# Rounding the high parts of the weights in a GpSimd DMA queue instead of on ScalarE

## The reference

```
h = concat(meta, x)
mix = hybrid_mixer(rmsnorm(h), ...)        # 16 stick-breaking heads, 4 retention heads, two gates, then @ w_out
h = h + rmsnorm(mix)
h = h + rmsnorm((silu(a) * b) @ w_ffn_out)  # a, b = split(rmsnorm(h) @ w_ffn_in), width 2816
...
second block: 5 input projections, a causal convolution of 3 taps and one of 31 taps,
layer norm, @ w_out_2, then a second SwiGLU of width 2816
```

## Time and profile before

| | before |
|---|---|
| device time, median of 3 runs | 2078.57 us (2076.77 to 2080.33) |
| span of the profiled execution | 2078.3 us |
| PE busy | 2016.7 us (97%) |
| DVE busy | 1095.9 us (53%) |
| ACT busy | 710.0 us (34%), of it 267.3 us high parts of weights |
| POOL busy | 14.6 us (1%) |
| DMA | 157.5 MB, 76 GB/s mean |

### The profile page before, as it was taken

The page is one execution under the profiler, slowest core; times in us unless marked ns, Lnnn a source line. Parts: engine busy times, 40 slices in busy tenths (PEclk is TensorE's granted clock), DMA queues, the critical chain, the costliest instruction groups (busy, mean ns, idle before and its releaser), DMA issues.

```text
span 2078.3 us, 25213 instructions
## 1 busy us (share of the span) xinstructions
PE 2016.7 (97%) x10194; PEld 1667.7 (80%) x10194; DVE 1095.9 (53%) x1346; ACT 710.0 (34%) x845; POOL 14.6 (1%) x10
## 2 busy tenths in 40 slices
PE   7999999989999999999999999999999999999996
PEld 6878888778989888887768888887898768888884
DVE  3454645544363544636564445454699664544445
ACT  5554655523332323224342222223333442222222
POOL 0000000000000000000000000000000000000000
PEclk9989999989999999999999999999999999999998
DMA  4010101012212222221312222222122112222221
GB/s 166 21 41 21 61 20 61 22 70 99 73 61 81 71 90 81 81 81 63 143 41 102 81 101 101 91 90 83 60 82 81 41 61 101 101 81 101 82 100 41
DMA packets 23475, 157.53 MB, mean 76 GB/s; under 512 B 2673, under 2 KB 3057, under 8 KB 5361
## 3 DMA queue, kind: packets, MB, share of 16 engines
q1 hardware_dynamic: 23408, 156.59, 21.7%
HBM read 154.48 MB, written 2.10 MB: 75 GB/s over the span
## 4 chain that ended last, share of the span: by engine, by line
PE 87%; DVE 7%; ACT 3%; issue 2%; DMA 0%; DVEq 0%; ACTq 0%
PE psum L463 27%; PE psum L464 27%; PE psum L465 26%; PE psum L595 2%; PE psum L517 2%; DVE z L1290 2%; DVE normed L1290 1%; DVE h L1319 1%; PE psum L583 1%; ACT w_hi L855 1%; ACT std L855 1%; DVE w_lo L1283 0%; PE psum L616 0%; DVE X_lo L1299 0%; PE psum L565 0%
## 5 line engine op out<-in xcount | busy, mean ns | idle before, releaser
L463 PE MATMUL psum<-X_hi,w_hi 128*128 128x512 f32 (+1 forms) x1632 | 607.2, 372 | 5.2 <-DVE X_lo L1299 5.0
L464 PE MATMUL psum<-X_lo,w_hi 128*128 128x512 f32 (+1 forms) x1632 | 603.4, 370 | 0.0
L465 PE MATMUL psum<-X_hi,w_lo 128*128 128x512 f32 (+1 forms) x1632 | 600.1, 368 | 0.0
L855 ACT ACTIVATE w_hi<-w_raw 128x2048 fp32r<-128x2048 f32 x140 | 267.3, 1909 | 423.8 <-PE psum L465 407.9
L1283 DVE TENSOR_TENSOR w_lo<-w_raw,w_hi 128x2048 fp32r<-128x2048 f32 x138 | 316.0, 2291 | 144.5 <-ACT w_hi L855 144.5
L463 PEld LDWEIGHTS psum<-X_hi,w_hi 128*128 128x128 f32 x1632 | 308.0, 189 | 69.1 <-issue 6.4
L464 PEld LDWEIGHTS psum<-X_lo,w_hi 128*128 128x128 f32 x1632 | 307.6, 188 | 54.8 <-issue 2.2
L465 PEld LDWEIGHTS psum<-X_hi,w_lo 128*128 128x128 f32 x1632 | 307.4, 188 | 53.7
L1428 DVE TENSOR_TENSOR acc<-acc,psum 128x512 f32<-128x512 f32 x216 | 142.1, 685 | 91.3 <-PE psum L465 91.3
L464 PE MATMUL psum<-M_lo,w_hi 128*128 128x512 f32 x352 | 139.1, 395 | 0.0
L465 PE MATMUL psum<-M_hi,w_lo 128*128 128x512 f32 x352 | 139.0, 395 | 0.0
(11 more groups left out here) (237 smaller groups left out, 2651.8 us busy)
## 6 DMA issues: line engine op xcount, KB each, us to landing
w_raw<-in_units SPq DMA_DIRECT2D x140, 1024.0 KB, 4.9
h<-in_xfm SPq DMA_DIRECT2D x4, 528.0 KB, 5.8
h<-in_xfm SPq DMA_DIRECT2D x1, 2112.0 KB, 7.5
decay<-in_dec SPq DMA_DIRECT2D x4, 512.0 KB, 4.8
out<-h SPq DMA_DIRECT2D x4, 512.0 KB, 2.8
rot<-in_consts SPq DMA_DIRECT2D x1, 528.0 KB, 11.2
acc<-in_consts SPq DMA_DIRECT2D x1, 448.0 KB, 8.7
vec<-in_vecs SPq DMA_DIRECT2D x1, 108.0 KB, 3.6
```

Of the source, the lines that this page charges most:

```text
L463: nc.tensor.matmul(dst, w2[0], x2[0], start=first, stop=False, skip_group_check=True)
L464: nc.tensor.matmul(dst, w2[0], x2[1], start=False, stop=False, skip_group_check=True)
L465: m = nc.tensor.matmul(dst, w2[1], x2[0], start=False, stop=last, skip_group_check=True)
L855: return nc.scalar.activation(out_, in_, f, **kw)
```

## The change

GpSimd now issues a DMA for every unit, from the same place in DRAM, with the float32r tile `w_hi` as its destination, so the DMA rounds on its way. It waits for nothing for units 0 and 1, and for the last strip of unit u - 2 for every later unit. ScalarE makes no high parts of weights any more: every `split_hi` and `first_hi` is gone. VectorE's `split_lo` waits for both loads of its unit. SyncE's load waits for the low part only. GpSimd's memsets stand between the new loads. The diff, cut where removals repeat:

```diff
@@ plan
-    start, u, s = {}, 0, 0
+    start, u, s, last = {}, 0, 0, []
     for name, kinds in phases:
         start[name] = (u, s)
         u += len(kinds)
-        s += sum(STRIPS[k] for k in kinds)
-    return start, u, s
+        for k in kinds:
+            s += STRIPS[k]
+            last.append(s)
+    return start, u, s, last
@@ build
-    w_hi_ready = sem("w_hi_ready")
+    w_hi_loaded = [sem("w_hi_loaded0"), sem("w_hi_loaded1")]
@@ sync
         def load(u, slot):
-            sync.wait_ge(w_hi_ready, u - 1)
             sync.wait_ge(w_lo_ready, u - 1)
@@ gpsimd
+        def load_hi(u):
+
+            if u > 1:
+                pool.wait_ge(strip_done, LAST_STRIP[u - 2])
+            pool.dma_start(w_hi[u % 2][:, :], units[u, :, :]).then_inc(w_hi_loaded[u % 2], 16)
+
+        def loads_hi(first, last):
+            for u in range(first, last):
+                load_hi(u)
+
         nc.gpsimd.memset(ones[:, :], 1.0).then_inc(ones_ready, 1)
+        loads_hi(0, 2)
         pool.wait_ge(x_lo_ready, DT)
         nc.gpsimd.memset(KM[:, :], 0.0).then_inc(memset_done, 1)
         pool.wait_ge(cmat_ready, 1)
         nc.gpsimd.memset(acc[:, :, :], 0.0).then_inc(memset_done, 1)
+        loads_hi(2, START["head0"][0] + 2)
 
         pool.wait_ge(strip_free, START["head0"][1])
         nc.gpsimd.memset(ret[:, :, :], 0.0).then_inc(ret_zero, 1)
-        for n in range(2):
+        done = START["head0"][0] + 2
+        for n, phase in enumerate(("ffn0", "ffn0_2")):
+            loads_hi(done, START[phase][0] + 2)
+            done = START[phase][0] + 2
             pool.wait_ge(post_done, (2 * n + 1) * DT)
             nc.gpsimd.memset(acc[:, :, :], 0.0).then_inc(acc_zero, 1)
+        loads_hi(done, N_UNITS)
@@ scalar
-        def split_hi(at, j):
-
-            act.wait_ge(w_loaded[at.ring(j)], 16 * (at.loads(j) + 1))
-            a(w_hi[at.ring(j)][:, :], w_raw[at.ring(j)][:, :], ACT.Copy).then_inc(w_hi_ready, 1)
-
...
-        def first_hi(u):
-            act.wait_ge(w_loaded[u], 16)
-            a(w_hi[u][:, :], w_raw[u][:, :], ACT.Copy).then_inc(w_hi_ready, 1)
...
@@ vector
         def split_lo(at, j):
 
-            dve.wait_ge(w_hi_ready, at.unit(j) + 3)
+            dve.wait_ge(w_loaded[at.ring(j)], 16 * (at.loads(j) + 1))
+            dve.wait_ge(w_hi_loaded[at.ring(j)], 16 * (at.loads(j) + 1))
             v.tensor_tensor(w_lo[at.ring(j)][:, :], w_raw[at.ring(j)][:, :], as_f32(w_hi[at.ring(j)][:, :]),
                             ALU.subtract).then_inc(w_lo_ready, 1)
@@ first_lo
-            dve.wait_ge(w_hi_ready, u + 1)
+            dve.wait_ge(w_loaded[u], 16)
+            dve.wait_ge(w_hi_loaded[u], 16)
```

More of the change, by code:

```diff
@@ L93, in plan @@
         u += len(kinds)
-        s += sum(STRIPS[k] for k in kinds)
-    return start, u, s
-START, N_UNITS, N_STRIPS = plan()
+        for k in kinds:
+            s += STRIPS[k]
+            last.append(s)
+    return start, u, s, last
+START, N_UNITS, N_STRIPS, LAST_STRIP = plan()
 class Place:
@@ L885, in norm @@
                 for k in range(DT):
-                    if k == 2 and n == 0:
-                        first_hi(0)
                     act.wait_ge(norm_scaled, DT * n + k + 1)
@@ L989, in quad_body @@
             value_hi(at, 1)
-            split_hi(at, 0)
             softplus(g + 1)
@@ L996, in quad_body @@
             softplus(g + 2)
-            split_hi(at, 1)
             meta_softplus(p + 1)
@@ L1001, in quad_body @@
                 strips(at, 11)
-                split_hi(at, 2)
             y_hi(0, p)
@@ L1010, in quad_body @@
             meta_weights(p + 1)
-            if has_next:
-                split_hi(at, nj)
         at = Place("quad_start")
@@ L1024, in _ @@
               as_f32(y[:, :, 0:32]).unsqueeze(2).broadcast_to([P, DT, 4, 32]), ACT.Copy).then_inc(quad_ready, 1)
-        first_hi(1)
         key_hi(0, at, 0, 0)
         query_hi(0, at, 1)
-        split_hi(at, 0)
         quad_body(Place("quad_first"), 0, False, True)
@@ L1050, in body @@
                         a(sig[:, c, 0:SEQ], strip_view(at.bank(2 * j + c), SEQ), ACT.Sigmoid).then_inc(strip_free, 1)
-                    split_hi(at, j)
             loop(act, 2, body, 2)
@@ L1074, in head_body @@
                             .then_inc(*r_act.step(f"VM_hi{n}"))
-                split_hi(at, n)
             act.wait_ge(r_dve.sem, r_dve.at("S3", i))
@@ L1086, in head_body @@
                         .then_inc(*r_act.step(f"g_sig{e}"))
-                split_hi(at, 2 + n)
             if has_next:
@@ L1100, in head_body @@
                 turned_hi("q", RQ_hi, SEQ, i + 1)
-                split_hi(at, 4)
             else:
                 gate_hi(at, 1)
-                split_hi(at, 4)
                 gate_hi(at, 2)
@@ L1139, in _ @@
             a(X_hi[:, k, META:FULL], acc[:, k, :], ACT.Copy).then_inc(m_split_hi, 1)
-            if k % 4 == 3:
-                split_hi(at, k // 4)
         def product_norm(phase, n):
@@ L1149, in ready @@
                     strips(at, k)
-                    split_hi(at, k // 2)
                 act.wait_ge(strip_free, at.strip(k) + 1)
@@ L1165, in gate_up @@
                         .then_inc(*f_act.step(f"sig{c}"))
-                split_hi(at, j)
                 strips(at, s + 3)
-                split_hi(at, j + 1)
                 act.wait_ge(f_dve.sem, f_dve.at("prod", i))
@@ L1177, in two @@
                     strips(at, 12 * m + 11)
-                    if not (final and m == 1):
-                        split_hi(at, 3 * m + 2)
             base = FF_PAIRS * n
@@ L1218, in _ @@
             take(at, 4 * half, FULL, ACT.Sigmoid, conv_sig, (c_dve.sem, c_dve.at("glu1")) if half else None)
-            split_hi(at, 2 * half)
             take(at, 4 * half + 2, FULL, ACT.Copy, glu_val, (c_dve.sem, c_dve.at("glu1")) if half else None)
-            split_hi(at, 2 * half + 1)
         at = Place("conv_a")
@@ L1225, in _ @@
                 take(at, 6 * half + 2 * j, n, ACT.Copy, dst, free if half else None)
-                if j < 2:
-                    split_hi(at, 3 * half + j)
             for t in (2 * half, 2 * half + 1):
@@ L1230, in _ @@
                 a(y2_hi[:, t, :], c_in[:, t % 2, 0:SEQ], ACT.Copy).then_inc(*c_act.step(f"y_hi{t}"))
-            split_hi(at, 3 * half + 2)
         at = Place("w_out2_a")
```

6 lines of the change are left out of this document (removed).

## The result

The changed kernel takes 2104.68 us, the median of 4 runs (2102.19 to 2106.80), against 2077.93 us for the kernel before in the same session: ratio 1.0130, 95% interval 1.0116 to 1.0145. It is 26.7 us slower, where +63 us were forecast. The profiled execution has a span of 2103.0 us.

A forecast was written before the change was run, and what follows sets the result against it. TensorE was taken as the bound, under way 97% of the span. 38 + 19.4 + 7 + 3.0 - 1.3 - 3 = +63 us on 2078.3 gave 2141 us; range 2086 to 2275, the forecast's own 2083 to 2195.

The forecast's parts named there:

- T: Time from GpSimd's wait to the landing of its 1 MB DMA; taken as 7.5 us, with ends 4.9 and 11.3.
- the row of the 2112 KB load: Profile row of a load that took 7.5 us, used for T because two unit loads would be in flight together.
- Part 1: FFN, 20 rounds: TensorE waits T - 5.6 us at the down unit's strip 7, +38 us in all.
- Part 2: Retention, 4 heads: each loses T - 2.45 - 0.2 = 4.85 us behind the late low part, +19.4 us.
- Part 3: Convolution: a late low part shifts the taps by 5.05 us and an earlier one adds 1.9 us, +7 us.
- Part 4: Norms: +3.0 us after the first w_out, -1.3 us in the two others, where ScalarE's copy is gone.
- Part 5: Start: VectorE no longer waits for ScalarE's first high part, -3 us; delay of x taken as 0, at most +3.
- At nothing: GpSimd's issues and waits, attention stages, single P units and SP's load triggers: priced at no cost, attention hiding T to 7-11 us.
- the rival of the ring: T above 8.8 us makes TensorE wait in every unit: 2273 us at T = 10, about 2380 at 11.3; chance 25%.
- its slope: FFN rounds and heads add about 26 us per us of T above 5.6, about 6 us per us below.
- The short-T rival: T at most 5 us, FFN rounds lose nothing and the kernel is not slower: 2075 to 2083 us; chance 14%.

The follow-up runs named there:

- the run with the longer T: The changed kernel with four small GpSimd memsets between its wait and each DMA of a high part: 2198.34 us, ratio 1.0583.
- the filler matmuls: The changed kernel with extra matmuls per head where TensorE stands still before the second gate unit: 2106.84 us with 20, 2101.81 us with 12.
- the fastest kernel: The changed kernel with VectorE's low parts reordered throughout, GpSimd's first two loads after x, and six more taps before the convolution's last low part: 2063.80 us, ratio 0.9939.
- its predecessor: The fastest kernel without the six more taps ahead of the convolution's last low part: 2070.14 us, ratio 0.9966.

## Why the prediction was right and wrong

**The sign and the mechanism held.** Slower was given 90%, by VectorE's program order behind a DMA that lands later than ScalarE's copy did. The runs show it by moving the low part alone.

**The step that failed is the size of T**, in the forecast's words "I take T = 7.5 us, by that row", the row of the 2112 KB load. The argument was that w_raw and w_hi are in flight together like one load of 2 MB. Measured: 5.65 us at most units, with w_raw unchanged at 4.9 us. The premise failed and not its price: the two issues were worked out with T = 7.5 itself, at 9.8 and 11.2 us after the strip. With the T that came, w_raw is issued 3.2 to 3.6 us ahead of w_hi and nearly landed. Where the issues did fall together, w_hi took 6.6 to 8.7 us, as the row of the 2112 KB load said. For the other units the nearer row was the one of the same size, 4.9 us; with GpSimd's 0.3 us and the time from the strip's end to the issue it gives the right T. The Trainium skill's page DMA: Bandwidth & Descriptors, section Anatomy of one DMA, gave an estimate of 4.4 us for this DMA, its section Bandwidth 6.15 us for the transfer alone; from issue to landing it took 5.2 us, between the two, and the measurement decides.

**Part 1** was built on a threshold of 5.6 us, and T came out at 5.65. That is why the 38 us became 1.9. The threshold itself was right: with T at 7.85 TensorE waits where it was said, by nearly the amount said.

**Part 2** had the right place and slack. Its formula gives 12 us at the measured T; 16.2 were measured. The forecast charged only the wait: TensorE's half clock after it adds 1.6 us a head, 6.4 in all, of which 0.7 comes back further on in each of the first three heads.

**Part 3** gives 3.2 at T = 5.65 and 5.0 came. At the late low part T was 7.3, the two issues being 0.55 us apart, and T - 2.45 is then 4.8. The wait and the chain of taps behind it were as told; the stall of 3.23 us on y_lo ahead of the stage's end, with half clock behind it, was overlooked.

**Part 4** was right: +0.8 and twice -1.8, which is the bound of 1.9 us named there. **Part 5** gave -3; the low part itself no longer waits, but x landed late (four pieces of 528 KB at 9.3 us, before 5.8), so the first unit began 1.65 us late and 1.1 us were left. The loads of x were the cost bounded by +3.

**"At nothing"** was wrong at two places: the end of the first FFN, where a down product follows the last round and its fifth strip needs VectorE within 5.6 us of the low part's release, so the slack is 5.6 - 2.3 - 0.7 = 2.6 us (4.6 us lost, 1.8 of it clock), and the last stage of the attention, where softplus stands behind the low part and T was 9.1 (3.5 us). The rest of the attention gained 2.5 us.

**The forecast was saved from a second error by the first.** At T = 7.85 its terms give +63 + 0.35 x 26 = +72 us; the run with the longer T measured +120. By these two, an estimate, T = 7.5 would have given some 40 us more than forecast, for the clock and the two places. It takes a delayed landing for a slow one, and whether slow loads that meet would lengthen each other further, as the rival of the ring had it, stays open.

**The range** held the time. The forecast's own upper end of 2195 us doesn't follow from its slope: T = 8.8 gives 63 + 1.3 x 26 = +97, 2175 us; nothing else used it. The short-T rival had the size of T nearly right and the sign wrong, as the heads need T under 2.65 us.

## What to carry to other kernels

When a value that a neighbour engine made in 2 us comes by a DMA that lands after 5.65 us, list everything that stands behind its consumer in program order, and move the consumer down by that difference, above all outside the steady loop: the ends, the first and the last rounds had the least slack here. Price a TensorE stall of near 3 us with the slower matmuls behind it (1.5 us here). Before pricing two loads as one, work out when each is issued with the short landing time too, and look for the places where the issues fall together. Freeing an engine off the path (255 us of ScalarE) paid only where its work stood in front of something that TensorE waited for, such as the squares of the norms (1.8 us each).

## What was not expected of the hardware

Behind the stalls of 2.7 to 2.9 us in the four heads and at the end of the first FFN TensorE was at a granted clock of 0.50 for about 3 us, behind the one of 3.23 us for about 7. The stall of 2.36 us in the last stage of the attention left the grant at 1.00. In the run with the longer T the twenty stalls of the FFN, 1.66 to 2.22 us long, were followed by a fall in twelve rounds, behind one of 1.75 us but not behind one of 1.90. So the length of a stall doesn't decide it alone. The Trainium skill, page TensorE: Matmul & The Clock Gate, section Part 1: The HAM clock gate, says that a hardware block sets the clock by how busy the engine has been lately, at one of two levels; the falls to 0.50 behind idle stretches and the 1.00 that the filler matmuls kept agree. In the attention stages the grant also fell in some rounds and not in others without any difference in the waits. The same stretch of two kernels with the same instructions there, the changed one and the fastest one, each with one wait of 0.6 us:

```profile
260.00:268.00 8.00, 7.43 (x32) 5.46 (x32) 2.23 (x2) 1.76 (x4) 0.53 (x1) 0.82 0.37 131
268.00:276.00 8.00, 8.00 (x32) 6.84 (x31) 5.21 (x9) 4.25 (x7) 0.00 (x0) 0.76 0.38 131
```

```profile
255.00:263.00 8.00, 7.44 (x41) 5.72 (x40) 1.88 (x2) 2.09 (x5) 0.53 (x1) 1.00 0.41 131
263.00:270.00 7.00, 7.00 (x39) 5.93 (x39) 5.56 (x9) 3.92 (x6) 0.00 (x0) 1.00 0.43 150
```

The two kernels differ by 2.2 us over such a round, and the profiled executions by about four of them: at the end of the attention's loop the fastest kernel was 12.9 us ahead of the kernel before, its predecessor 9.3, the changed kernel 3.6. Part of the last gain (6.3 us in the median, where 3.4 were expected) may be of this kind; in the profiled executions 3.5 of the 8.3 us between the two fastest kernels lie ahead of the heads, where both have the same instructions. What decides it stays open.

Two 1 MB loads issued 2 us or more apart landed in the median as alone (5.2 and 4.9 us), while issued within 1 us of each other GpSimd's took 6.6 to 8.7 us. At the start, where x, the constants and four units came together, the constants landed after 13.0 and 15.8 us instead of 8.7 and 11.2.
